# A hybrid decoder step: fp32r state update, early merge, and a group norm computed by halves

## The chip, the cores and the metric

The kernel runs on one core of one Trainium2 chip. The metric is the device time of one execution in microseconds. The engines are named as in the profile: PE is TensorE (PEld its weight loads), DVE is VectorE, ACT is ScalarE, POOL is GpSimd, SP is SyncE, which issues most DMAs.

## What is computed

One inference step of one decoder layer for 256 prompt tokens and 8 x 4 sample tokens (288 columns in all), D_MODEL 2048:

```
x += 0.5 * swiglu(rmsnorm(x));  x += mix(rmsnorm(x)) @ w_out;  x += 0.5 * swiglu(rmsnorm(x));  y = rmsnorm(x)

mix:  q, k, v, f, z, xbc, dt, g, u = split(xn @ w_in)
      att  = forgetting attention(q, k, v)                       # 512 features
      y, state = ssd_scan(x, dt, a, B, C, h0)                    # 16 heads x 64, state 128, 2 groups
      yg   = (y * silu(z)) in 2 groups of 512
      yg   = yg * rsqrt(mean(yg * yg) + eps) * ssd_norm          # the group norm
      lru  = rglru(u) * gelu(g)                                  # 512 features
      out  = [att | yg | lru] @ w_out
```

For the sample tokens the scan starts from `state_ssd` (8 sequences x 16 heads x 64 x 128, 4 MB), and the new states are an output.

## The kernel before

The residual x lies transposed in SBUF, 16 blocks of 128 features by 288 tokens. Every weight tile of 128 columns is loaded in fp32 (`wraw`, four slots), rounded to fp32r by ACT (`whi`), its remainder computed by DVE (`wlo`), and multiplied in three fp32r products per k-block (`products`, L792 to L794), so 48 products for 16 k-blocks. The activations are split in the same way (`xn_hi`/`xn_lo`, for the second half of the mixer `m_hi`/`m_lo`).

The mixer has 41 input tiles (`in`), then 16 output tiles of part 0 (k-blocks of attention and LRU, held in blocks 0 to 3 and 12 to 15 of `xn_hi`), 24 products each, then 16 of part 1 (the eight normed SSM blocks). The order is written by hand: the list `STEPS` is walked by each engine in its own program, and each step issues what that engine has to do for it. Beside the tiles stand these steps:

- `turn_x` transposes the conv output (`xsT`) to token rows (`xsn`, `bnat`), in three blocks of tokens; block 2 holds the 32 sample tokens, copied into two row groups (`turn_copies`, L824).
- `scores` makes the masked C B products (`cbm`), `hist` turns the conv histories, `ssd` h makes head h's decay matrix (`lseg` on DVE and ACT, `mseg` on POOL) and, for odd h, the output y of two heads back (`ssd_y`).
- `merge` rounds attention and LRU into `xn_hi`/`xn_lo`; `decay_s` makes the sample rows of `bexp` (B masked by sequence).
- `unit` i turns 4 x 2 heads of the old state (`ht`, L817), computes the update of unit i-1 (L1084, K = 32 rows, fp32) and its contribution to y (L1088). ACT copies `h0t`, DVE writes `snew`, SP stores it and loads the state four units on (`load_h0`).
- `gate_prompt` multiplies y by silu(z) on DVE and squares it on ACT; `sum_prompt` sums the squares over features on PE with a matrix of ones (L1102).
- `carry` finishes the sample columns; `groups` 0 to 3 compute mean, root (Ln, then Exp on ACT, then a Newton step on DVE), norm and rounding for both groups at once.
- `decay_x` and `state` make the prompt's final state.

PE writes the side products of all steps to three PSUM banks in turn: `JOB` numbers them in the order of STEPS, and `claim` for job j waits until job j-3 was read by its reader.

The old state's four slots (`h0`) lie in `xn_lo` blocks that the input tiles use, and SP loads them only after `merge` (wait for `merged` 8). The lines of the steps after the input tiles are, before:

```
    STEPS += [("hist", 2), ("hist", 3)] + ssd(2) + tile()
    STEPS += ssd(2) + [("in", IN_TILES), ("merge", 0)]
    STEPS += [("decay_s",)]
    for n, h in enumerate(heads):
        j, odd = h // 2 - 2, h % 2
        STEPS += [("ssd", h), ("unit", next(units)), ("sum_prompt" if odd else "gate_prompt", j)]
        STEPS += out() if n % 3 != 2 else []
```

## Time and profile before

| | us |
|---|---|
| three timed runs | 2293.6, 2294.14, 2295.75 (median 2294.14) |
| the profiled execution's own time | 2286.04 |
| its span, first to last instruction | 2284.9 |
| PE busy in the span | 2219.1 (97%) |
| DVE busy | 1194.9 (52%) |
| ACT busy | 820.2 (36%) |
| POOL busy | 155.9 (7%) |
| mean granted TensorE clock | 0.990 of full speed |

The profiled execution and the timed runs are different executions; the first is a little shorter than the median of the second. A matmul's duration in the timeline includes its way through the array, so products that follow each other overlap: what one costs is the distance from its start to the next one's. An fp32 matmul stands in two records. The granted clock of a window is 1.00 for 2.4 GHz all through and 0.50 for 1.2 GHz all through. The profile calls the state's slots `h`.

### The profile page before, as it was taken

Reading aid. Unit: us, or ns where it says so; the run is one execution under the profiler, and the core shown is the slowest. Engines: PE = TensorE matmul, PEld = TensorE weight load, DVE = VectorE, ACT = ScalarE, POOL = GpSimd, SP = SyncE. Lnnn points to the kernel's source line nnn. Section 1 sums busy time; section 2 is a strip of 40 time slices with the busy share of each in tenths; the row PEclk is TensorE's granted clock in tenths of the full one; section 3 lists DMA queues with packets and bytes.
Section 4 is the critical chain, followed back from the end, with each engine's and each line's share of the span. In section 5 each row is a group of like instructions: output and inputs, shape, how many; then the busy total and the mean of one; then the engine's idle time right before and its main releaser. Section 6 shows DMA issues by size and latency. Waiting matters only on the chain.

```text
span 2284.9 us, 41945 instructions
## 1 busy us (share of the span) xinstructions
PE 2219.1 (97%) x17040; PEld 2154.8 (94%) x17040; DVE 1194.9 (52%) x1541; ACT 820.2 (36%) x798; POOL 155.9 (7%) x221
## 2 busy tenths in 40 slices
PE   6999999999999999999999899899999999999998
PEld 6999999999999999988888679899999999999997
DVE  5555445554445457556436666545444554445554
ACT  5333233333233343344343435433333333233333
POOL 2410000000000030100000202000000000000022
PEclk8999999999999999999999999999999999999999
DMA  7665665656666566656975555665566656566552
GB/s 190 172 169 153 166 167 163 167 159 170 166 166 164 148 163 198 184 165 187 287 220 176 165 148 172 169 166 163 158 167 165 168 157 167 161 166 166 158 158 93
DMA packets 696130, 386.51 MB, mean 169 GB/s; under 512 B 18216, under 2 KB 677836, under 8 KB 695192
## 3 DMA queue, kind: packets, MB, share of 16 engines
q1 hardware_dynamic: 691528, 378.79, 60.0%
q0 software_dynamic: 4112, 5.94, 1.0%
q8 instruction: 75, 1.23, 0.2%
q10 hardware_dynamic: 384, 0.30, 0.0%
q14 instruction: 31, 0.25, 0.0%
HBM read 373.86 MB, written 11.13 MB: 168 GB/s over the span
## 4 chain that ended last, share of the span: by engine, by line
PE 88%; DVE 4%; SPq 2%; ACT 2%; issue 2%; DMA 1%; ACTq 0%; POOL 0%; DVEq 0%; POOLq 0%
PE bank L792 28%; PE bank L794 28%; PE bank L793 28%; DVE wlo L1524 1%; SPq L488 1%; PE bank L817 1%; SPq L487 1%; PE bank L1084 1%; ACT whi L1208 1%; PE bank L999 0%; DMA kpage<-cache_k 0%; DMA vpages<-cache_v 0%; DVE xn_lo L1514 0%; PE bank L945 0%; PE bank L944 0%
## 5 line engine op out<-in xcount | busy, mean ns | idle before, releaser
L792 PE MATMUL bank<-xn_hi,whi 128*128 128x288 f32 x3536 | 1057.2, 299 | 22.3 <-DVE xn_lo L1514 10.8
L793 PE MATMUL bank<-xn_hi,wlo 128*128 128x288 f32 x3536 | 1047.9, 296 | 0.0
L794 PE MATMUL bank<-xn_lo,whi 128*128 128x288 f32 x3536 | 1044.2, 295 | 0.0
L1524 DVE TENSOR_TENSOR wlo<-wraw,whi 128x2048 fp32r<-128x2048 f32 (+3 forms) x341 | 726.5, 2130 | 391.6 <-ACT whi L1208 391.2
L1208 ACT CAST whi<-wraw 128x2048 fp32r<-128x2048 f32 (+3 forms) x341 | 605.4, 1776 | 748.0 <-PE bank L794 740.9
L792 PEld LDWEIGHTS bank<-xn_hi,whi 128*128 128x128 f32 x3536 | 667.6, 189 | 29.9 <-DVE wlo L1524 17.7
L794 PEld LDWEIGHTS bank<-xn_lo,whi 128*128 128x128 f32 x3536 | 670.7, 190 | 0.0
L793 PEld LDWEIGHTS bank<-xn_hi,wlo 128*128 128x128 f32 x3536 | 668.8, 189 | 0.3
L794 PE MATMUL bank<-h_lo,whi 128*128 128x288 f32 x1376 | 407.0, 296 | 0.0
L792 PE MATMUL bank<-h_hi,whi 128*128 128x288 f32 x1376 | 406.1, 295 | 0.0
L793 PE MATMUL bank<-h_hi,wlo 128*128 128x288 f32 x1376 | 404.9, 294 | 0.0
L793 PEld LDWEIGHTS bank<-h_hi,wlo 128*128 128x128 f32 x1376 | 259.1, 188 | 0.0
L792 PEld LDWEIGHTS bank<-h_hi,whi 128*128 128x128 f32 x1376 | 258.3, 188 | 0.0
L794 PEld LDWEIGHTS bank<-h_lo,whi 128*128 128x128 f32 x1376 | 258.0, 188 | 0.0
L1222 ACT ACTIVATE sg<-sg 128x288 f32<-128x288 f32 x86 | 38.3, 445 | 422.8 <-DVE sg L1532 422.8
L1558 DVE SCALAR_TENSOR_TENSOR xT<-bank,xT 128x288 f32 (+1 forms) x108 | 49.5, 458 | 207.3 <-PE bank L794 207.3
L1532 DVE TENSOR_TENSOR sg<-bank,rs 128x288 f32<-128x288 f32 x86 | 39.4, 458 | 179.6 <-PE bank L794 179.5
L632 POOL COPY ssum<-sq 128x288 f32<-128x288 f32 x3 | 3.9, 1297 | 1415.3 <-ACT sq L1199 1415.3
L1539 DVE TENSOR_TENSOR hm<-bank,rs 128x288 f32<-128x288 f32 x86 | 39.3, 457 | 114.0 <-PE bank L794 114.0
L639 POOL TENSOR_TENSOR ssum<-ssum,sq 128x288 f32<-128x288 f32 x45 | 68.3, 1519 | 134.8 <-ACT sq L1199 134.8
L1547 DVE TENSOR_TENSOR h_lo<-hm,h_hi 128x288 f32 (+1 forms) x86 | 39.4, 459 | 9.0
L817 PE MATMUL bank<-ident,kpage 128*128 128x128 f32 x256 | 35.0, 280 | 6.8 <-DMA kpage<-cache_k 3.9
(355 smaller groups left out, 1136.1 us busy)
## 6 DMA issues: line engine op xcount, KB each, us to landing
wraw<-ffn_w_gate SPq DMA_DIRECT2D x86, 1024.0 KB, 5.9
wraw<-ffn_w_up SPq DMA_DIRECT2D x86, 1024.0 KB, 5.8
wraw<-ffn_w_down SPq DMA_DIRECT2D x64, 960.0 KB, 5.5
wraw<-w_in SPq DMA_DIRECT2D x40, 1024.0 KB, 6.3
wraw<-ffn_w_down SPq DMA_DIRECT2D x32, 832.0 KB, 5.2
kpage<-cache_k SPq DMA_DIRECT2D x64, 256.0 KB, 3.0
vpages<-cache_v SPq DMA_DIRECT2D x64, 256.0 KB, 4.0
wraw<-w_out SPq DMA_DIRECT2D x64, 256.0 KB, 3.4
```

The source lines that it names most:

```text
L639: pool.tensor_tensor(ssum[:], ssum[:], sq[:, odd, :], ALU.add).then_inc(sem("summed"), 1)
L792: pe.matmul(out, hi, rhs_hi, start=k == 0, stop=False)
L793: pe.matmul(out, lo, rhs_hi, start=False, stop=False)
L794: return pe.matmul(out, hi, rhs_lo, start=False, stop=k == nk - 1)
L817: return pe.transpose(out, src, ident[0:n, 0:n])
L1208: act.copy(tile_ap(whi, (base + j) % 2, nk), tile_ap(wraw, slot, nk)).then_inc(sem("hi_done"), 1)
L1222: act.activation(sg[:, par, :], sg[:, par, :], ACT.Silu).then_inc(sem("silu_done"), 1)
L1524: dve.tensor_tensor(tile_ap(wlo, s, nk), tile_ap(wraw, (base + j) % LOADS, nk), tile_ap(whi, s, nk).bitcast(F32), ALU.subtract).then_inc(s ...
L1532: dve.tensor_tensor(sg[:, par, :], bank[bk][:, 0:N], rs[:, 2, :], ALU.mult).then_inc(sem("scaled"), 1)
L1539: dve.tensor_tensor(hm[:, par, :], bank[bk][:, 0:N], rs[:, 2, :], ALU.mult).then_inc(sem("up_scaled"), 1)
L1547: dve.tensor_tensor(h_lo[:, bass.ds(slot, 1), :].rearrange("p o t -> p (o t)"), hm[:, par, :], h_hi[:, bass.ds(slot, 1), :].rearrange("p o ...
L1558: dve.scalar_tensor_tensor(out=xk, in0=bank[bk][:, 0:N], scalar=scale, in1=xk, op0=ALU.mult, op1=ALU.add).then_inc(sem("x_added"), 1)
```

## The change

Four things:

1. The sample rows of x and B are split into a rounded part and a remainder, each in its own row group of 32 (x: high, high, low, low; B: high, low, high, low), so that the update of the state is one fp32r product over 128 rows (`xw`, `bsp`, `masked_b`) in place of an fp32 one over 32.
2. The last input tile takes the outer k-blocks first (`LAST_K`), and `merge` stands ahead of heads 2 and 3; it waits for `outer_used`, which counts after the first eight k-blocks.
3. The old state's slots and `bexp` lie in the halves of `wraw` that output tiles leave free; SP loads them once the last input tile's remainder is done.
4. The group norm is done by halves. Group 0's `ys`, mean, root and norm (`ys_scale`, `ys_turn`, `mean`, `norm`, `round`) stand amid the units, group 1's at the end. POOL adds the squares of a group's four blocks, and PE multiplies one sum instead of four. ACT takes a square root, and DVE a reciprocal, in place of Ln and Exp.

Units begin two heads later, so three more of them follow each other behind the last head.

```diff
-    STEPS += ssd(2) + [("in", IN_TILES), ("merge", 0)]
+    STEPS += [("merge", 0)] + ssd(2) + [("in", IN_TILES)]
...
-    STEPS += [("decay_s",)]
+    NORM0 = {10: [("ys_scale", 0)], 11: [("ys_turn", 0)], 12: [("mean", 0)], 13: [("norm", 0)]}
     for n, h in enumerate(heads):
         j, odd = h // 2 - 2, h % 2
-        STEPS += [("ssd", h), ("unit", next(units)), ("sum_prompt" if odd else "gate_prompt", j)]
-        STEPS += out() if n % 3 != 2 else []
-    for u, more in zip(units, ([("gate_prompt", 7)], [("sum_prompt", 7)] + out(), [])):
-        STEPS += [("unit", u)] + more
-    STEPS += [("carry",)] + out() + [("groups", 0), ("decay_x",)] + out() + [("groups", 1)] + out() + [("groups", 2)] + out()
-    STEPS += [("state", 0), ("state", 1), ("groups", 3)] + out()
+        STEPS += [("ssd", h)] + ([("unit", next(units))] if n >= 2 else []) + [("sum_prompt" if odd else "gate_prompt", j)]
+        STEPS += out() if n < 2 or n % 3 != 1 else []
+        STEPS += [("decay_s",)] if n == 0 else NORM0.get(n, [])
+    STEPS += [("unit", next(units)), ("gate_prompt", 7), ("round", 0)] + out() + [("unit", next(units)), ("sum_prompt", 7)]
+    STEPS += [("unit", next(units))] + out() + [("unit", next(units)), ("decay_x",)] + out() + [("unit", u) for u in units]
+    STEPS += [("ys_scale", 1)] + out() + [("ys_turn", 1), ("state", 0)] + out() + [("mean", 1), ("state", 1)] + out()
+    STEPS += [("norm", 1), ("round", 1)]
...
SP:
-                        sp.wait_ge(sem("merged"), 8)
+                        sp.wait_ge(sem("lo_done"), IN0 + IN_TILES)
...
POOL:
+            elif what == "sum_prompt" and i % 4:
+                pool.wait_ge(sem("y_squared"), i + 1)
+                if i % 4 > 1:
+                    pool.wait_ge(sem("prompt_summed"), i // 4 * 3 + i % 4 - 1)
+                s = zT[:, i // 4 * 4, 0:NP_]
+                pool.tensor_tensor(s, s, zT[:, i, 0:NP_], ALU.add).then_inc(sem("prompt_summed"), 1)
...
PE:
+        LAST_K = [0, 1, 2, 3, 12, 13, 14, 15] + list(range(4, 12))
...
-                for k in range(KT):
+                for n, k in enumerate(LAST_K if t == IN_TILES - 1 else range(KT)):
...
+                    if t == IN_TILES - 1 and n == 7:
+                        last.then_inc(sem("outer_used"), 1)
...
-                if not (first and part == 0 and n < 2):
+                if first and part == 0 and n < 2:
+                    pe.wait_ge(sem("in_taken"), IN_TILES)
+                else:
                     pe.wait_ge(sem("x_added"), XO0 + part * KT + n + it4 - 1)
...
+                    if first and part == 1 and n == 0 and k in (0, 4):
+                        pe.wait_ge(sem("merged"), k + 12)
...
-                            m = turn_copies(to[:, c * P:(c + 1) * P], src, 1 if i < 2 else 2)
+                            m = turn_copies(to[:, c * P:(c + 1) * P], src, 1 if i < 2 else 4)
...
-                        pe.wait_ge(sem("bexp_ready"), 2)
-                        pe.matmul(to[:, :], xsn[SX, 2, c * P:(c + 1) * P], bexp[SX, c // 4, b0:b0 + 4, :],
+                        pe.wait_ge(sem("bexp_ready"), 4)
+                        pe.matmul(to[:, :], xw[:, c * P:(c + 1) * P], masked_b(c // 4, u % 2),
...
+                elif what == "mean":
+                    to = claim(pe, "mean", i)
+                    pe.wait_ge(sem("prompt_summed"), 3 * i + 3)
+                    pe.matmul(to[:, 0:NP_], ones[:], zT[:, 4 * i, 0:NP_], start=True, stop=True)
+                    pe.wait_ge(sem("gsq_ready"), i + 1)
+                    pe.matmul(to[:, NP_:N], ones[:], gsq[:, i, :], start=True, stop=True).then_inc(side_done("mean", i), 1)
...
ACT:
-                    act.wait_ge(sem("w_used"), IN0 + IN_TILES)
+                    act.wait_ge(sem("outer_used"), 1)
...
-                    act.activation(grs[:, 1], grs[:, 0], ACT.Ln).then_inc(sem("groot_step"), 1)
-                    act.wait_ge(sem("groot_step"), 1)
-                    act.activation(grs[:, 1], grs[:, 1], ACT.Exp, scale=-0.5).then_inc(sem("groot_step"), 1)
+                elif what == "mean":
+                    copied(act, "mean", i)
+                    act.activation(grs[:, 1, :], grs[:, 0, :], ACT.Sqrt).then_inc(sem("groot_step"), 1)
+                elif what == "round":
+                    if i == 0:
+                        act.wait_ge(sem("mseg_ready"), H_SSD)
+                        take(act, "y", 7)
+                    else:
+                        for q in range(2):
+                            act.wait_ge(sem(f"snew_stored{q}"), 16 * ND)
+                    act.wait_ge(sem("yn_done"), i + 1)
+                    act.copy(m_hi[:, 4 * i:4 * i + 4, :], zT[:, 4 * i:4 * i + 4, :]).then_inc(sem("m_rounded"), 1)
...
DVE:
+            def split_sample_x():
...
+                decay = nat[:, 2, 96 + 32:96 + 48]
+                dve.tensor_tensor(by_head(xw[:]), by_head(xsn[:, 2, :]), spread(decay, HD), ALU.mult)\
+                    .then_inc(sem("xw_step"), 1)
+                dve.tensor_copy(bsp[:], bnat[:, 2, :]).then_inc(sem("xw_step"), 1)
+                dve.wait_ge(sem("xw_step"), 1)
+                dve.tensor_tensor(by_head(xsn[low, 2, :]), by_head(xsn[low, 2, :]), spread(decay[low], HD), ALU.mult)\
+                    .then_inc(sem("xw_step"), 1)
+                dve.wait_ge(sem("xw_step"), 2)
+                for r in (1, 3):
+                    dve.tensor_tensor(bsp[SQ[r], :], bnat[SQ[r], 2, :], bsp[SQ[r], :].bitcast(F32), ALU.subtract)\
+                        .then_inc(sem("xw_step"), 1)
+                dve.wait_ge(sem("xw_step"), 3)
+                dve.tensor_tensor(xw[low, :], xsn[low, 2, :], xw[low, :].bitcast(F32), ALU.subtract)\
+                    .then_inc(sem("xw_step"), 1)
+                dve.wait_ge(sem("xw_step"), 6)
...
+                elif what == "mean":
...
+                    dve.tensor_scalar(v, src[:, 0:N], 1.0 / 512, EPS, ALU.mult, ALU.add).then_inc(side_read("mean", i), 1)
+                    dve.wait_ge(sem("groot_step"), i + 1)
+                    chain(dve.reciprocal(y, y))
+                    chain(dve.tensor_tensor(z, y, y, ALU.mult))
+                    chain(dve.scalar_tensor_tensor(out=z, in0=z, scalar=-0.5, in1=v, op0=ALU.mult, op1=ALU.mult))
+                    chain(dve.scalar_tensor_tensor(out=z, in0=z, scalar=1.5, in1=y, op0=ALU.add, op1=ALU.mult))
```

Where this puts the instructions is seen in the order on DVE at three places (the number after L is the line, before or after the change). First, behind the third block of `turn_x`; the parts of `xsn` and `bnat` are the turned rows, `cbm` the masked scores. Before:

```order
L1860 TENSOR_TENSOR xsn<-bank,nat 64x512 x2
L1865 COPY bnat<-bank 64x256
L1867 COPY cpad<-xsT 128x2x8x4
L1871 TENSOR_TENSOR cbm<-bank,tri 128x384
L1872 TENSOR_TENSOR cbm<-bank,tris 32x32
```

In the changed kernel:

```order
L1903 TENSOR_TENSOR xsn<-bank,nat 128x512 x2
L1908 COPY bnat<-bank 128x256
L1706 TENSOR_TENSOR xw<-xsn,nat 128x1024
L1708 CAST bsp<-bnat 128x256
L1710 TENSOR_TENSOR xsn<-xsn,nat 64x1024
L1714 TENSOR_TENSOR bsp<-bnat,bsp 32x256 x2
L1717 TENSOR_TENSOR xw<-xsn,xw 64x1024
L1912 COPY cpad<-xsT 128x2x8x4
L1916 TENSOR_TENSOR cbm<-bank,tri 128x384
L1917 TENSOR_TENSOR cbm<-bank,tris 32x32
```

Six instructions of the split now stand ahead of the first masked score.

Second, on DVE around the merge; `xn_lo<-attT` and `xn_lo<-gT` are its two subtractions, `lseg` a head's decay (three instructions), `zT<-bank` the read of an input tile. Before, from head 3 on:

```order
L1889 TENSOR_SCALAR lseg<-bank,nat 128x256
L1889 TENSOR_SCALAR lseg<-bank,nat 128x128
L1889 TENSOR_SCALAR lseg<-bank,nat 32x32
L1895 SCALAR_TENSOR_TENSOR xsT<-xsT,dcol,bank 128x288
L1647 TENSOR_TENSOR zT<-bank,rs 128x288
L1876 TENSOR_TENSOR xn_lo<-attT,xn_hi 128x1152
L1879 TENSOR_TENSOR xn_lo<-gT,xn_hi 128x1152
L1910 TENSOR_TENSOR xsn<-xsn,nat 32x1024
L1912 TENSOR_TENSOR bexp<-bnat,bmask 32x1024 x2
```

In the changed kernel, from the weight of output tile 0 to the read of the last input tile:

```order
L1539 TENSOR_TENSOR wlo<-wraw,whi 128x1024
L1921 TENSOR_TENSOR xn_lo<-attT,xn_hi 128x1152
L1924 TENSOR_TENSOR xn_lo<-gT,xn_hi 128x1152
L1934 TENSOR_SCALAR lseg<-bank,nat 128x256
L1934 TENSOR_SCALAR lseg<-bank,nat 128x128
L1934 TENSOR_SCALAR lseg<-bank,nat 32x32
L1934 TENSOR_SCALAR lseg<-bank,nat 128x256
L1934 TENSOR_SCALAR lseg<-bank,nat 128x128
L1934 TENSOR_SCALAR lseg<-bank,nat 32x32
L1940 SCALAR_TENSOR_TENSOR xsT<-xsT,dcol,bank 128x288
L1664 TENSOR_TENSOR zT<-bank,rs 128x288
```

The subtractions stand ahead of heads 2 and 3, and the read of the last input tile behind them all. The four products of `bexp` follow after head 4, the gating of y 0 and one more weight.

Third, on DVE, the first group's norm in the changed kernel; `grs` holds mean and root, `snew` is a unit's new state. Before, these `grs` steps (L1953 to L1963, 576 columns for both groups) stand after the last unit.

```order
L1999 TENSOR_SCALAR grs<-bank 128x288
L2001 RECIPROCAL grs<-grs 128x288
L2002 TENSOR_TENSOR grs<-grs 128x288
L2003 SCALAR_TENSOR_TENSOR grs<-grs 128x288
L2004 SCALAR_TENSOR_TENSOR grs<-grs 128x288
L1940 SCALAR_TENSOR_TENSOR xsT<-xsT,dcol,bank 128x288
L1967 SCALAR_TENSOR_TENSOR snew<-wraw,dec,bank 128x128 x4
L2007 SCALAR_TENSOR_TENSOR zT<-xsT,params,grs 128x288 x4
L1967 SCALAR_TENSOR_TENSOR snew<-wraw,dec,bank 128x128 x4
L1992 TENSOR_TENSOR xsT<-xsT,zT 128x256
L2013 TENSOR_TENSOR m_lo<-zT,m_hi 128x1152
L1637 TENSOR_TENSOR xT<-xT,bank 128x288
```

The read of y 7 (`xsT<-xsT,dcol,bank`) stands behind the whole root, and norm and rounding ahead of the addition of an output tile and the weight after it.

## Rows read from the trace of the kernel before

**Rows 1.** The page, part 1: busy us, share of the span and instructions
```profile
PE 2219.1 (97%) x17040; PEld 2154.8 (94%) x17040; DVE 1194.9 (52%) x1541; ACT 820.2 (36%) x798; POOL 155.9 (7%) x221
```

**Rows 2.** Waits of PE, 1225 to 1440 us: us in total, times, longest
```profile
PE bank L817 <- DMA h<-state_ssd: 10.4, 1, 10.4
...
PE bank L1096 <- DVE ys L1930: 2.2, 1, 2.2
PE bank L792 <- DVE wlo L1524: 2.0, 1, 2.0
```

**Rows 3.** Windows: length; busy of PE, PEld, DVE, ACT, POOL; granted clock; DMA
```profile
1268.00:1272.50 4.50, 4.42 (x20) 4.46 (x21) 2.37 (x6) 2.36 (x5) 1.21 (x2) 0.52 0.81 234
1353.00:1361.00 8.00, 7.74 (x38) 7.77 (x39) 3.72 (x7) 2.63 (x3) 0.00 (x0) 0.58 0.61 172
1367.00:1371.50 4.50, 4.50 (x22) 4.50 (x23) 4.36 (x7) 0.00 (x0) 0.00 (x0) 0.62 0.39 117
```

**Rows 4.** Timeline of PE: start, duration (us), line, out<-in, count [idle before]
```profile
1236.35 2.38 PE L824 MATMUL bank<-ident,xsT 128*32 128x128 f32 x40
...
1240.72 1.06 PE L817 MATMUL bank<-ident,histO 128*27 128x128 f32 x8
...
1249.50 0.29 PE L792 MATMUL bank<-xn_hi,whi 128*128 128x288 f32 x1
...
1255.88 0.43 PE L1057 MATMUL bank<-cshl,hot 128*128 128x288 f32 x2
...
1268.08 1.09 PE L817 MATMUL bank<-ident,h 128*128 128x128 f32 x4 [10.40 <-DMA h<-state_ssd]
1268.82 0.59 PE L792 MATMUL bank<-xn_hi,whi 128*128 128x288 f32 x1
...
1275.51 1.12 PE L1084 MATMUL bank<-bexp,xsn 32*128 32x512 f32 x2
1276.56 0.42 PE L1088 MATMUL bank<-h0t,cpad 128*32 128x128 f32 x8
1276.92 0.70 PE L1102 MATMUL bank<-zT,ones 128*128 128x256 f32 x2
...
1277.58 0.29 PE L793 MATMUL bank<-xn_hi,wlo 128*128 128x288 f32 x1
...
1382.26 0.37 PE L792 MATMUL bank<-m_hi,whi 128*128 128x288 f32 x1 [0.34 <-issue]
```

**Rows 5.** DVE, groups by form, 1233 to 1384: busy us, mean ns | idle before
```profile
L1524 DVE TENSOR_TENSOR wlo<-wraw,whi 128x1024 fp32r<-128x1024 f32 x18 | 22.6, 1258 | 11.7 <-ACT whi L1208 11.7
...
L1967 DVE SCALAR_TENSOR_TENSOR zT<-xsT,params,grs 128x288 f32<-128x288 f32 x8 | 3.5, 511 | 0.0
...
L1974 DVE TENSOR_TENSOR m_lo<-zT,m_hi 128x1152 fp32r<-128x1152 f32 x2 | 2.6, 1352 | 0.0
...
L1905 DVE TENSOR_TENSOR xsn<-xsn,nat 128x1024 f32<-128x1024 f32 x2 | 2.4, 1218 | 0.0
```

**Rows 6.** Timeline of DVE and POOL, 1251 to 1256 us
```profile
1251.73 3.39 POOL L738 TENSOR_TENSOR mseg<-lseg,cbm 128x384 f32<-128x384 f32 x4 [33.90 <-ACT lseg L1374]
...
1253.15 1.87 DVE L1524 TENSOR_TENSOR wlo<-wraw,whi 128x1024 fp32r<-128x1024 f32 x1 [1.88 <-ACT whi L1208]
```

**Rows 7.** DMA issues, 1225 to 1440 us: count, KB each, us to landing
```profile
xT<-x_save SPq DMA_DIRECT2D x1, 2304.0 KB, 8.5
```

**Rows 8.** Timeline of DVE around the first score mask
```profile
1239.80 0.56 DVE L1871 TENSOR_TENSOR cbm<-bank,tri 128x384 f32<-128x384 f32 x1 [0.35 <-PE bank L1050]
1240.27 0.17 DVE L1872 TENSOR_TENSOR cbm<-bank,tris 32x32 f32<-32x32 f32 x1
```

**Rows 9.** DVE, groups by form, whole span: the wide reciprocal
```profile
L1585 DVE RECIPROCAL ps<-ps 72x288 f32<-72x288 f32 x1 | 1.9, 1949 | 0.0
```

**Rows 10.** Timeline of ACT around the group norm's root
```profile
1362.74 1.28 ACT L1396 ACT_TABLE_LOAD   x1
1364.04 0.69 ACT L1396 ACTIVATE grs<-grs 128x576 f32<-128x576 f32 x1
```

166 lines of the change are left out of this document (74 added, 92 removed).

## Prediction

> **What bounds the kernel now.** I read the page first: TensorE (PE) is busy 97% of the span [rows 1], so time is to be had only where PE waits, runs at its lower clock, or does work that can be made cheaper. The changed code acts only in the second half of the mixer, from the turning of the third token block (about 1236 us) to the first output tile that uses the normed heads (1382.26). The waits of PE in that stretch come next [rows 2]: 10.4 us for the first load of the old state, 2.2 us for `ys`, 2.0 us for a rounded weight. Then the windows [rows 3]. After each of the three waits the granted clock reads 0.52, 0.58 and 0.62, which means that PE ran at the 1.2 GHz level for most of it. Window length times (1 - granted) gives what each cost: 4.5 x 0.48 = 2.2, 8.0 x 0.42 = 3.4, 4.5 x 0.38 = 1.7 us. So the waits of before cost 14.6 us and the slow stretches behind them 7.3 us. Last I read PE's own order [rows 4], with both ends of the stretch, for the price of each kind of work. Where a product follows a product, start to start is its cost: an input tile of 48 products takes 6.38 us (1249.50 to 1255.88), 0.133 each, and an output tile of 24 takes 3.2.
>
> **The change, part by part** (minus is faster).
>
> *State update as one fp32r product.* Per unit, L1084 takes 1.05 us (1275.51 to 1276.56) for 512 columns in fp32 [rows 4]. In fp32r, 0.133 us for 288 columns scales to 0.24. I take 0.24, since more rows in the contraction cost nothing in the 128-row tiles; the other bound is no gain, 1.05. 16 x 0.81 = -13.0. Not all of it comes through: two even heads are followed by an odd one with no tile between, and there the odd head's products wait for the side bank that ScalarE empties, as just met before; I give back 0.85 twice, +1.7.
>
> *Sums of squares on GpSimd.* Eight L1102 products go, two come. One costs about 0.53: 1276.92 to 1277.58, less one 0.133 product [rows 4]. 6 x 0.53 = -3.2, and +0.4 for two small sample products where one stood: -2.8. GpSimd's six sums lie beside other work: two heads' mseg took it 3.39 us [rows 6], a sum is narrower than one of the mseg products, and a head now takes PE about 4 us. Vector's (DVE's) weight subtraction L1524 took 1.87 us beside GpSimd's 3.39 us of mseg, against a mean of 1.26 [rows 5, 6], so six sums could slow DVE by 0 to 3.9 us. I take 0, since DVE has slack per head in the steady part. The Trainium skill (GPSIMD Engine Reference, key points) says that GpSimd shares its memory interfaces with VectorE and contends with instructions that have two SBUF inputs, which speaks against this move; it also puts elementwise work at about twice VectorE's time. By that rule the sum would be up to 3.9 worse; the 1.87 agrees with it.
>
> *Merge before heads 2 and 3, state loads free of it.* Before, head 4 ends at 1257.68 and PE idles until 1268.08 [rows 4]; its first output tile starts at 1268.8, 19.3 after the start T of the last input tile (1249.50). Now the outer k-blocks come first in that tile, done at T+3.2, and ScalarE, free of the next weight at T+3.6, rounds twice until T+5.7. DVE ends that weight at T+5.5 [rows 6], subtracts twice (1.35 each) until T+8.1, and only then does heads 2 and 3 (0.8 each), y 0 and the read of the tile (0.4 each): T+10.5, for which the output tile now waits. PE is free at about T+8, so a wait of 2.7 stands in place of 10.4: 19.3 - 10.5 = -8.8. The low clock behind it stays (+0.1). The loads of the state now queue behind the 2304 KB copy of x, 8.5 us [rows 7]; both end near T+14, and the first unit is at T+20: hidden.
>
> *Three-part split of the sample rows.* Each of ten chunks is turned into four row groups instead of two. Two copies cost 0.23 (2.38 us for ten) [rows 4]; four narrow products into four groups take 0.36 (L1088, 1276.56 to 1276.92): +1.3; the bounds are 0 and 2.4. DVE gets a chain ahead of the score masks: three products like L1905, 1.22 each [rows 5], and three of 256 columns, some 0.3 each by size: 4.6 us. The second history turn on PE needs the bank of score mask 0. That mask waited 0.35 and ended at 1240.44 [rows 8], 0.8 before that turn started (half-way through the row at 1240.72). So PE moves by 1.3 + 4.6 - 1.2 = +4.7, 3.2 of it idle, and I add a slow stretch of +2.0, between the 1.7 and 3.4 seen. The later weights are 3 us early and stay covered.
>
> *The mask product.* Four of 512 columns, 0.6 each, now stand on DVE after the weight of tile 1 and before head 5. Before, 3.5 us of it hid in the 10.4 wait. Tile 2's weight comes 2.0 later than PE wants it: +2.0, clock +1.7, and 0.2 at tile 1: +3.9.
>
> *First norm amid the units.* On DVE: scale and add, then ScalarE's root (0.5 with hand-over), a reciprocal of 1.95 (the 72x288 row of L1585 [rows 9]; cost goes by columns), three steps of about 0.5, as L1967 [rows 5]: 4.4 us in which DVE does nothing else. Behind it is the read of y 7, whose bank the next turn of the state needs: PE waits 3.0. Then four norm products, a rounding of 1.15 on ScalarE and a 1.35 subtraction [rows 5] stand before the weight of tile 11: 1.8 more, and clock 1.7: +6.5.
>
> *Tail.* The `ys` and weight waits and their clock go, -9.3. In their place: 0.8 at tile 13; and after the second mean product DVE needs 4.4 for the root, 1.6 for an addition and a weight, 2.0 norm, ScalarE 1.1, DVE 1.4, in all 10.4, against PE's 1.9 (state) + 3.2 (last tile) + 1.6 (first four k-blocks, already normed) = 6.7. Wait 3.7, clock 1.7: net -3.1.
>
> The removed logarithm pair had a table load of 1.28 between its two steps, 1362.74 to 1364.04 [rows 10]; with a square root none stands on the chain. The Trainium skill (ScalarE: Activation LUTs, What ACT_TABLE_LOAD costs) counts 2.66 us for each switch, a drain included. The row has the next activation right behind the 1.28, so here the drain is not seen, and by the page's figure the old chain would have been 1.4 longer; the sum uses the row.
>
> **Sum:** -13.0 + 1.7 - 2.8 - 8.7 + 6.7 + 3.9 + 6.5 - 3.1 = -8.8, about -9. The profiled execution took 2286.04 (span 2284.9), so it would take 2277; the three timed runs have a median of 2294.14, 8 above it, and -9 makes that 2285.
>
> **Rivals.**
> 1. *The new waits are dearer* (no change). I count five or six waits of 2 to 4 us, in place of one long and two short. If each is followed by 3.4 of lost clock and not 1.7 to 2.0, +8: 2293. For: one of the three did. Against: two did not.
> 2. *The waits are shorter* (faster still). If only the merge and the last root make PE wait long enough for the clock, the split, mask, and norm stretches give back 2.0 + 1.7 + 1.7 + some 2 of wait: 2278. For: steady heads leave DVE 2 us per three heads.
> 3. *The clock stays low between neighbouring waits* (slower). From the merge wait to tile 2 PE has 9.7 us of work between two waits, from the norm wait to tile 11 another 7, and the input tile after the split is 6.4. If all of it runs at 1.2 GHz, it takes twice as long and costs 23 where I counted 7.6: +15.5, and 2301. It decides from 13.6 us lost beyond the count on, that is, only if nearly every low stretch lasts until the next wait. Against: two of three ended within 4.5 us [rows 3].
> 4. *The fp32r product is no cheaper.* Then -8.8 + 13.0 - 1.7 = +2.5: 2297, inside what counts as the same by half of its chance. Against: every weight product of the kernel is fp32r at 0.133.
> The Trainium skill (TensorE: Matmul & The Clock Gate, What's actually happening) calls the lower clock the default, released by activity, which is the ground of rivals 1 and 3; its figures are not used.
>
> **How the numbers follow.** What this kernel's measurement tells from no change is about 0.2%, 4.6 us. Forecast 0.58 (about 2280 to 2289, all faster); rival 2 0.14; rival 1 0.18, mostly within 4.6 us; rival 3 0.06; rival 4 0.04. Faster 0.72, same 0.20, slower 0.08. The range leaves out rivals 3 and 4 and the ends: low 2277, from rival 2, high 2293, from rival 1 and the bounds of the turning (+1.1) and of GpSimd's contention.
>
> **What would show it.** State updates of about 0.24 us start to start; mean products twice; PE's long wait for the load of the old state gone, one of 2 to 3 us before output tile 0; a new PE wait of about 3 before the second history turn; a wait at the turn of the state near head 17 on the y bank; a wait of about 3.7 before the fifth k-block of the first second-half tile. The mixer from 1249.50's tile to that tile should take 117 us, not 132.8. I am wrong if the split costs PE nothing or twice 6.7, or if windows behind the waits keep a granted clock near 0.5 for over 8 us.

## The result, and the profile after

| | us |
|---|---|
| the changed kernel, 20 runs | median 2285.41 (2279.64 to 2293.02) |
| the kernel before, 20 runs beside them | median 2290.27 (2285.99 to 2297.80) |
| ratio of the two, with its 95% interval | 0.9975 (0.9965 to 0.9984), that is 5.7 us less (3.7 to 8.0) |

The forecast of 2285 and "faster" came true; the size of the gain did not quite. The forecast counted 9 us down from 2294.14, the median of three runs. The twenty runs put the kernel before at 2290.27, and the change took off 5.7.

The profiled executions of the two kernels have the same span, 2284.9 us, and still the stage that the change touches is shorter. From here on *the stage* is the way from the first turning of the convolution's output (the first of its three token blocks) to the first product of the second feed-forward. It contains every instruction that the change moves. Before, it took 203.2 us (1233.30 to 1436.48), after it 195.1 (1237.55 to 1432.67): 8.1 less.

The rest of the span, where PE runs the same work, was 8.1 us longer in this one execution. It is the clock: outside the stage running below full clock cost PE 6.1 us before and 15.7 after, with its waits equal and its work the same within 1.6 (the mean granted clock of the whole span was 0.990 and 0.986). Such differences are common here: in thirteen profiles with this same code ahead of the stage, its start lay anywhere from 1230.6 to 1242.5. So the experiments below are read by two things, the stage and the ratio of many runs.

The two do not agree fully. The runs give 5.7 us (3.7 to 8.0) where the stage gives 8.1, and of the twelve kernels below eleven also gain less by the runs than by the stage, by 0.5 to 4.7 us. The kernel before has one profile only, so whether its stage was long in it, or the changed kernels lose time elsewhere, stays open. Against each other the changed kernels are on firmer ground.

The page of the changed kernel, part 1: busy us, share of the span and instructions.

```profile
PE 2214.6 (97%) x17066; PEld 2159.1 (94%) x17066; DVE 1204.8 (53%) x1555; ACT 818.9 (36%) x798; POOL 161.1 (7%) x227
```

PE is busy 4.5 us less than in [rows 1], DVE 9.9 more, POOL 5.2 more (six sums of 0.73, the rest longer `mseg` products). The waits of PE in the stage of the changed kernel (us in total, times, longest) stand where [rows 2] stood:

```profile
PE bank L803 <- DVE wlo L1539: 4.8, 5, 2.1
PE bank L830 <- DVE cbm L1917: 3.8, 1, 3.8
PE bank L830 <- DVE xsT L1940: 3.1, 1, 3.1
PE bank L803 <- DVE m_lo L2013: 2.6, 1, 2.6
PE bank L892 <- ACT h0t L1398: 1.5, 2, 0.7
PE bank L803 <- issue: 1.2, 1, 1.2
PE bank L1103 <- DVE lseg L1934: 1.2, 3, 0.6
PE bank L1076 <- DVE lseg L1934: 1.1, 1, 1.1
```

The one long wait for the load of the old state and the two short ones have become fifteen shorter ones, 19.3 us in all against 14.6 (14.9 with one of 0.3 that names `issue`). Twelve of the fifteen name DVE. The windows of the changed kernel (columns as in [rows 3]) show the granted clock behind five of them, and the recovery after the last:

```profile
1249.40:1252.40 3.00, 2.99 (x13) 2.86 (x14) 0.88 (x3) 1.90 (x2) 0.00 (x0) 0.51 0.08 21
1269.70:1273.00 3.30, 3.28 (x14) 3.30 (x15) 1.31 (x4) 3.27 (x3) 1.45 (x4) 0.52 1.19 305
1282.50:1287.00 4.50, 4.43 (x22) 4.44 (x23) 2.77 (x7) 2.36 (x5) 2.01 (x4) 0.62 0.00 0
...
1339.60:1345.00 5.40, 4.74 (x28) 4.12 (x29) 4.68 (x15) 1.23 (x3) 0.15 (x1) 0.68 0.36 99
...
1378.50:1384.00 5.50, 5.50 (x30) 5.50 (x31) 3.08 (x4) 1.82 (x3) 0.40 (x1) 0.69 0.32 95
1384.00:1390.00 6.00, 6.00 (x48) 6.00 (x47) 3.62 (x7) 3.51 (x6) 1.39 (x2) 1.00 0.52 152
```

Length times (1 - granted) gives 1.5, 1.6, 1.7, 1.7 and 1.7 us: five stretches near the 1.2 GHz level, each over within about 5 us, 8.2 in all against the 7.3 of before. Forecast were five of 1.7 to 2.3, 9.4 in all. So the stage splits in three: the waits grew by 4.6 (15.2 to 19.7, counting every one over 0.15 us but the last), the low clock took 0.9 more, and PE's own work, which is what remains of 203.2 and 195.1, fell by 13.5, from 180.7 to 167.2. PE gained more by cheaper work than it lost in waits. *Work* below always means this remainder.

Where the 8.1 us come from, by five marks on PE (T is the start of the last input tile):

| us | before | after | difference | forecast |
|---|---|---|---|---|
| first turning to T | 16.20 | 21.55 | +5.35 | +6.7 |
| T to the first output tile | 19.32 | 10.62 | -8.70 | -8.7 |
| first output tile to the first product with normed heads | 113.44 | 104.33 | -9.11 | -12.2 |
| from there to the second feed-forward | 54.22 | 58.62 | +4.40 | +5.4 |
| the stage | 203.18 | 195.12 | -8.06 | -8.8 |

Each interval came out within 1.4 us but the third, 3.1 off, where the update, the sums, the mask and the first norm meet. The experiments take these apart.

### The profile page after: what moved, and what is told of

The parts are those of the page before. It is cut to its first block, busy times and chain, and to the rows that moved or that the text cites. A ratio compares the mean times of both kernels' runs of the same rounds, so it can differ in the third digit from the quotient of the medians.

```text
span 2284.9 us, 42031 instructions
## 1 busy us (share of the span) xinstructions
PE 2214.6 (97%) x17066; PEld 2159.1 (94%) x17066; DVE 1204.8 (53%) x1555; ACT 818.9 (36%) x798; POOL 161.1 (7%) x227
## 4 chain that ended last, share of the span: by engine, by line
PE 85%; DVE 6%; SPq 3%; ACT 2%; issue 2%; DMA 1%; ACTq 0%; POOL 0%; DVEq 0%; POOLq 0%
PE bank L803 28%; PE bank L805 27%; PE bank L804 27%; DVE wlo L1539 1%; SPq L492 1%; SPq L491 1%; ACT whi L1221 1%; PE bank L830 1%; DMA vpages<-cache_v 0%; PE bank L1018 0%; DMA kpage<-cache_k 0%; DVE snew L1967 0%; DVE lseg L1934 0%; PE bank L1185 0%; DVE xn_lo L1529 0%
## 5 line engine op out<-in xcount | busy, mean ns | idle before, releaser
L803 PE MATMUL bank<-m_hi,whi 128*128 128x288 f32 x128 | 38.8, 303 | 3.7 <-DVE m_lo L2013 2.6
```

What stands on the lines that cost most here:

```text
L803: pe.matmul(out, hi, rhs_hi, start=nth == 0, stop=False)
```

## Experiments

All run as changes of the changed kernel (195.1 us, ratio 0.9975). Every ratio is against the kernel before, from runs side by side; before ran at medians of 2289.06 to 2290.41. Two rows that differ by less than about 0.0015 (3.4 us) are not told apart by the runs alone. The stage comes from one profile each: in e3, e4, e5, e7 and e9 0.7 to 1.3 us of it lie ahead of T, at the same waits, and are the clock of that execution.

| run | stage | ratio, 95% interval |
|---|---|---|
| e1, split behind the scores | 189.9 | 0.9953 (0.9937 to 0.9969) |
| e2, each update product twice | 198.3 | 0.9978 (0.9965 to 0.9990) |
| e3, first mean one step later | 197.7 | 0.9987 (0.9976 to 0.9998) |
| e4, update product in fp32 | 199.4 | 1.0004 (0.9993 to 1.0015) |
| e5, sums back on PE | 197.2 | 0.9989 (0.9980 to 0.9998) |
| e6, root by logarithm | 194.8 | 0.9975 (0.9965 to 0.9984) |
| e7, merge behind the heads | 196.9 | 0.9975 (0.9964 to 0.9987) |
| e8, update all as before | 198.9 | 0.9991 (0.9977 to 1.0006) |
| e9, e4 and e7 together | 201.7 | 1.0002 (0.9988 to 1.0015) |
| e10, e1 with the mask in halves | 188.1 | 0.9952 (0.9938 to 0.9966) |
| e13, its second half a step earlier | 188.7 | 0.9950 (0.9932 to 0.9968) |
| e14, and the root apart | 190.2 | 0.9947 (0.9931 to 0.9963) |

One of the twelve runs of e14 took 4306.15 us at a full granted clock. It is left out of its ratio, and its cause is not known.

**The split (e1).** In the changed kernel DVE makes the three parts of x before the score masks. Timeline of DVE in the changed kernel:

```profile
1243.74 1.23 DVE L1706 TENSOR_TENSOR xw<-xsn,nat 128x1024 fp32r<-128x1024 f32 x1
1244.88 0.29 DVE L1708 CAST bsp<-bnat 128x256 fp32r<-128x256 f32 x1
1245.20 1.22 DVE L1710 TENSOR_TENSOR xsn<-xsn,nat 64x1024 f32<-64x1024 f32 x1
1246.45 0.86 DVE L1714 TENSOR_TENSOR bsp<-bnat,bsp 32x256 fp32r<-32x256 f32 x2
1247.35 1.22 DVE L1717 TENSOR_TENSOR xw<-xsn,xw 64x1024 fp32r<-64x1024 f32 x1
...
1248.72 0.55 DVE L1916 TENSOR_TENSOR cbm<-bank,tri 128x384 f32<-128x384 f32 x1
1249.18 0.17 DVE L1917 TENSOR_TENSOR cbm<-bank,tris 32x32 f32<-32x32 f32 x1
```

The chain takes 1243.74 to 1248.57, 4.8 us (forecast 4.6), and the mask behind it is what PE waits for. PE's timeline there, in the changed kernel:

```profile
1240.60 2.39 PE L837 MATMUL bank<-ident,xsT 128*32 128x128 f32 x80
1242.92 2.13 PE L1069 MATMUL bank<-xsT 128*128 128x256 f32 x12
1244.98 0.62 PE L830 MATMUL bank<-ident,histO 128*27 128x128 f32 x4
1249.41 1.05 PE L830 MATMUL bank<-ident,histO 128*27 128x128 f32 x4 [3.81 <-DVE cbm L1917]
```

e1 moves the call, and nothing else:

```
 turn_x, third block (DVE):
-                    if i == 2:
-                        split_sample_x()
 scores (DVE), after the masks:
+                    split_sample_x()
```

> The three-part split moves on VectorE from ahead of the masked scores to behind them, so that the second history turn no longer waits for it. Stage here and below: from the first turn of the conv output (1233.30 us before, 1237.55 in the changed kernel) to the first product of the second feed-forward (1436.48 and 1432.67): 203.2 us before, 195.1 changed. Theory 1 (the split's only price is the 3.8 us wait and the low clock of 2.3 us after it, some 1.5 lost; behind the scores VectorE waits anyway, 2.4 and 2.7 us): the wait goes, stage 190 (-5.3), total about 0.2% under the changed kernel, near 0.995 of the kernel before. Rival (the split is on VectorE's path wherever it stands): the wait moves to the last input tile's weight or to heads 0 and 1, and the stage stays within 1.5 us of 195.

Measured: stage 189.9, first turning to T 16.22, as the theory had it. The wait for `cbm` is gone from PE's waits, and nothing waits for the split at its new place. So 5.2 us were spent for an order that nothing asked for: the first reader of the parts is the mask product on DVE at 1276.35, 28 us after the chain ended. The ratio of the runs says the same, 0.9953 for 0.9975, 5.0 us.

**The price of the update product (e2).**

```
+                        pe.matmul(to[:, :], xw[:, c * P:(c + 1) * P], masked_b(c // 4, u % 2), start=True, stop=True)
                         pe.matmul(to[:, :], xw[:, c * P:(c + 1) * P], masked_b(c // 4, u % 2), start=True, stop=True)
```

> Each of the 16 fp32r state updates is issued twice into the same bank; the result is the same. The changed kernel's trace shows 0.41 us from the start of a 512-column update to the start of the next product, where the sum on record had 0.24. Theory 1 (0.41 is what such a product costs): 16 x 0.41 = 6.6, less what disappears in waits for the h0t copy and for heads' decay (some 1.5), stage 200 (+5). Rival (0.24 is the price of the product, the rest is a fixed gap to the fp32 products behind it, paid once): 16 x 0.22 = 3.5, less 1, stage 197.5 (+2.5).

Timeline of PE in e2, one unit (start, duration):

```profile
1289.30 0.47 PE L1103 MATMUL bank<-bexp,xw 128*128 128x512 f32 x1
1289.62 0.39 PE L1105 MATMUL bank<-bexp,xw 128*128 128x512 f32 x1
1289.93 0.42 PE L1109 MATMUL bank<-h0t,cpad 128*32 128x128 f32 x8
```

A unit in the changed kernel, and one before (turn of the state, update, its contribution to y):

```profile
1301.42 0.60 PE L830 MATMUL bank<-ident,wraw 128*128 128x128 f32 x4
1301.77 0.48 PE L1103 MATMUL bank<-bexp,xw 128*128 128x512 f32 x1
1302.18 0.42 PE L1107 MATMUL bank<-h0t,cpad 128*32 128x128 f32 x8
...
1280.77 0.60 PE L817 MATMUL bank<-ident,h 128*128 128x128 f32 x4
1281.30 1.12 PE L1084 MATMUL bank<-bexp,xsn 32*128 32x512 f32 x2
1282.35 0.42 PE L1088 MATMUL bank<-h0t,cpad 128*32 128x128 f32 x8
```

Two products take 0.63 us from the first start to that of the fp32 products behind them (1289.30 to 1289.93), one takes 0.41 (1301.77 to 1302.18). So the second costs 0.22, the rival's price, and the forecast's 0.24 for a product among its like was about right. The other 0.19 of the 0.41 come once, at the passage to the fp32 products. Against that the update now starts 0.35 after the turn ahead of it (1301.42 to 1301.77) and before it started 0.53 after it. From the turn to the products behind the update a unit took 1.58 and takes 0.76, 0.82 less.

PE's work grew by 3.6 (0.22 to 0.24 a unit). The waits gave back 2.0: the two for `h0t` fell from 0.74 to 0.53 each, the one for the y bank from 3.1 to 2.7, and most of the short ones for `lseg` went. The low stretch behind the y bank was twice as long in this execution and took 1.5 more, which makes the 3.2 that reached the stage. It lies between theory and rival, nearer the rival. In the runs e2 is 0.7 us slower than the changed kernel (0.9978 for 0.9975), inside both intervals.

**The update in fp32 (e4).** Same operands, same 128 rows, no fp32r:

```
-                        pe.matmul(to[:, :], xw[:, c * P:(c + 1) * P], masked_b(c // 4, u % 2),
+                        pe.matmul(to[:, :], xw[:, c * P:(c + 1) * P].bitcast(F32),
+                                  masked_b(c // 4, u % 2).bitcast(F32),
```

> Only the 16 products of the state update lose their fp32r form: they run as plain fp32 over the same 128 rows and 512 columns, and compute the same. Theory (the cheaper product carries 10 us of the stage): each goes from 0.31 to 0.41 us back to about 1.05, so the stage from the first turn of the convolution's output to the first product of the second feed-forward grows from 195.1 by 16 x 0.64 to 0.74 = 10 to 12 us, to 205 to 207. Rival (the time stood under cover of the vector engine, and the saving was small): the stage grows by under 5 us, to 200 at most.

Measured: the product takes 0.95 to 1.06, and with a slower start behind the turns PE's work is 10.4 us more from the first output tile to the first normed product. The stage grew by 4.3, 1.0 of it ahead of T, so 3.3 are the update's: the rival, by this one execution. Where 10.4 went shows in the waits of PE in e4:

```profile
PE bank L803 <- DVE wlo L1540: 3.8, 3, 2.1
PE bank L830 <- DVE cbm L1918: 3.8, 1, 3.8
PE bank L803 <- DVE m_lo L2014: 2.6, 1, 2.6
PE bank L830 <- DVE xsT L1941: 2.3, 1, 2.3
...
PE bank L1103 <- DVE lseg L1935: 0.8, 2, 0.6
```

The waits for `h0t` (1.5) are gone, those for `wlo` are 1.0 shorter, for the y bank 0.9, for `lseg` 0.5: 3.8 by their hundredths. The rest is clock. The windows of e4 behind tile 2 and behind the y bank, where the changed kernel had 0.62 and 0.68:

```profile
1284.50:1289.00 4.50, 4.49 (x41) 4.16 (x41) 2.76 (x7) 2.37 (x5) 1.98 (x4) 1.00 0.00 0
1344.80:1350.30 5.50, 5.48 (x42) 4.53 (x43) 4.08 (x13) 1.97 (x4) 0.74 (x1) 1.00 0.51 135
```

Length times (1 - granted) these two low stretches had cost the changed kernel 1.7 us each. 10.4 - 3.8 - 3.4 = 3.2, against 3.3 seen. So part is cover: DVE and ACT set the pace among the units once the product is cheap, and 3.8 of the 10.4 us go into waits for them. The other part is the clock of this execution and no property of the dear product: e9 has the same product and the same wait of 2.3 us for the y bank, and a low stretch behind it. The runs agree: e4's ratio is 1.0004 for 0.9975, 6.6 us more, which is 10.4 - 3.8 with the clock left out; their intervals allow 3 to 10.

**The update all as before (e8):** fp32, 32 rows of contraction, two copies in the turning, no split.

```
-            pe.matmul(to[:, :], xw[:, c * P:(c + 1) * P], masked_b(c // 4, u % 2),
+            pe.matmul(to[:, :], xsn[SX2, 2, c * P:(c + 1) * P], masked_b(c // 4, u % 2)[SX2].bitcast(F32),
...
```

> The state update is done as in the kernel before (plain fp32 products over 32 rows, two copies in the turning, x unsplit), all else as in the changed kernel; the result is the same. Theory (as e4_update_fp32 showed, two thirds of the dearer products lie under waits for VectorE and ScalarE, and the split's 5.3 us before the last input tile is gone as in e1_split_late): from the changed kernel's 195.1 the stage goes by -5.3 + 4.3 to 194, within 1.5 of it. Rival (the update's 10 us count in full): the stage is 200 or more.

Measured 198.9, 1.1 short of the rival and 4.9 above the theory, which took over e4's low stage. Both expectations missed. The split's 5.3 went as in e1; against e1 it is 9.0 more in the stage and 8.7 by the ratios. That is what the cheap update is worth against the one of before, both without the split in the way: 11.8 us of PE's work, less 1.5 that go into waits and 1.4 of clock. It is more than e4 tells, in part since the 32-row product of before is dearer than e4's (below). From the third output tile to the first normed product e8 took 100.7 us, the changed kernel 91.5, e4 94.8. The 6 us between e8 and e4, with the same arithmetic, are for the most part two stretches of low clock that e4 did not have. Windows of e8 at tile 2 and behind the y bank:

```profile
1279.40:1284.00 4.60, 4.54 (x23) 4.55 (x24) 2.81 (x7) 2.36 (x5) 2.01 (x4) 0.63 0.00 0
1341.80:1348.50 6.70, 6.70 (x27) 4.48 (x28) 4.69 (x14) 2.69 (x4) 0.73 (x1) 0.51 0.49 133
```

They cost 1.7 and 3.3 us. The waits ahead of them are 2.2 and 2.1 us; in e4 waits of 2.1 and 2.3 at the same places had nothing behind them. The 32-row product takes 1.05 each time where the 128-row one mostly took 0.95, and its start behind the turns 0.1 more. What decides whether the clock falls after a wait of 2 us these runs do not settle.

**The sums of squares (e5).**

```
 POOL:
-                pool.tensor_tensor(s, s, zT[:, i, 0:NP_], ALU.add).then_inc(sem("prompt_summed"), 1)
 PE, each prompt block:
+                    pe.matmul(bank[4][:, g * NP_:(g + 1) * NP_], ones[:], zT[:, i, 0:NP_], start=i % 4 == 0, stop=i % 4 == 3)
...
```

> Only the sums of squares of the prompts' columns go back to TensorE (six products with ones), out of GpSimd; the result is the same. Theory (the forecast's term of 2.8 us): each product takes about 0.44 to 0.46 us on TensorE, so the stage grows from 195.1 by 2.6 to 2.8, to about 197.8. Rival (GpSimd's sums slow VectorE beside them and give that back): the stage stays within 1 us of 195.1, and VectorE's busy time in it falls by 1 us or more.

Measured 197.2, +2.1, by the ratios +3.2 (0.9989 for 0.9975): nearer the theory. PE's work grew by 2.6, 0.43 for each of six sums. 0.7 of the stage's 2.1 lie ahead of T, and against that the waits for `wlo` are 0.9 shorter. POOL's sums do not slow DVE: the 34 subtractions for `wlo` took 1308 ns on average in the changed kernel's stage and 1306 in e5's, and DVE was busy 138.5 and 138.6 us. What contends is the pair of `mseg` products, and these stand in both kernels. Groups of DVE by form in the changed kernel, 1262 to 1374 (busy us, mean ns | idle before):

```profile
L1992 DVE TENSOR_TENSOR xsT<-xsT,zT 128x256 f32<-128x256 f32 x8 | 6.0, 750 | 1.0 <-ACT zT L1284 1.0
```

The gate product of y took 416 ns before (L1946), 750 now, 749 in e5 and 504 in e4. It slows not through the sums but because, with the cheap update, it falls beside POOL's `mseg`: four of the eight took 1.07 to 1.10 us (the first on DVE at 1295.27, POOL's pair at 1295.07), the others 0.40 to 0.43. The Trainium skill (GPSIMD Engine Reference, Specifications) says that the two engines contend where VectorE's instruction has two SBUF inputs; this product has, and the trace agrees.

**The merge (e7).**

```
-    STEPS += [("merge", 0)] + ssd(2) + [("in", IN_TILES)]
+    STEPS += ssd(2) + [("in", IN_TILES), ("merge", 0)]
```

> The merge stands behind heads 2 and 3 again, all else as changed (outer k-blocks first, state loads early, mask products late). Theory 1 (the order buys what stood before the merge on ScalarE: heads, table load, silu): the two subtractions end 15.3 after the start of the last input tile, as before, and output tile 0 starts there and not at 10.6: stage 200 (+4.7). Rival (the gain at the merge came from the state load and the mask products alone, which before stood between 15.3 and 19.3, and the read of the last input tile holds the output tile anyway): stage within 1 of 195.

Measured: stage 196.9, +1.8, where the theory had +4.7 and the rival less than 1. T to the first output tile is 14.2 instead of 10.6, so the early merge is worth 3.6 of the 8.7 there. The other 5.1 came without it; what else was changed at this place is the state's load, which no longer waits for the merge, and the mask product, which moved behind it. No run parts these two. Of the 3.6 only 1.8 are left at the end of the stage, and 1.0 of that lies ahead of T and has nothing to do with the merge. The rest went behind the first output tile: in e7 the waits for `wlo` at tiles 1 and 2 are smaller, none and 0.8 in place of 0.8 and 2.0. Waits of PE in e7:

```profile
PE bank L803 <- DVE xn_lo L1921: 6.0, 1, 6.0
...
PE bank L803 <- DVE wlo L1539: 2.8, 4, 1.1
```

In the runs no difference is left: both ratios are 0.9975, with room for 3 us either way.

**Two undone together (e9).** The edits of e4 and e7.

> Two parts undone together: the update's products as plain fp32 over 128 rows (as e4_update_fp32) and the merge of h back behind the first two heads and the last input tile (as e7_merge_behind_heads). Theory (each alone costs 4.3 and 1.8 us of the stage, most of it hidden by other waits; together they use up cover at different places, so the two add up): 195.1 + 6.1 = 201.2, within 1.5. Rival (both were hidden behind the same waits, and with both gone it shows): 204 or more.

201.7 against 201.2 by adding, the theory: their losses lie at different places. By the ratios (1.0002) it is as e4 alone, which agrees with a merge worth nothing.

**The first norm (e3, e6).**

```
 e3:
-    NORM0 = {10: [("ys_scale", 0)], 11: [("ys_turn", 0)], 12: [("mean", 0)], 13: [("norm", 0)]}
+    NORM0 = {10: [("ys_scale", 0)], 11: [("ys_turn", 0)], 13: [("mean", 0), ("norm", 0)]}
 e6:
-                    act.activation(grs[:, 1, :], grs[:, 0, :], ACT.Sqrt)
+                    act.activation(grs[:, 1, :], grs[:, 0, :], ACT.Ln)
+                    act.activation(grs[:, 1, :], grs[:, 1, :], ACT.Exp, scale=-0.5)
 ...
-                    chain(dve.reciprocal(y, y))
```

> The first group's mean and root move behind head 17 and its unit, so that VectorE reads y 7 and writes a new state before the 4.4 us root. Theory 1 (the 3.1 us wait is a matter of order: the y bank stands behind the root): that wait goes, the weight of tile 11 comes at most 1.5 later, stage 193 (-2). Rival (VectorE has too much work in these steps, whatever the order): the wait turns up at the weights of tiles 10 and 11, stage within 0.7 of 195.

> Only the root of the group norm is taken as before, by a logarithm and an exponential on ScalarE, in place of a square root and VectorE's reciprocal. Theory (the reciprocal's 1.95 us is what holds the y bank of tile 7): the chain from the mean to the first read of that bank is 0.45 + 1.28 (a table load) + 0.45 = 2.2 us in place of 0.45 + 1.95 = 2.4, where the load is not hidden, and 0.9 where it is: the wait of 3.1 us for that bank falls to 1.6 to 2.9, stage 193.6 to 195. Rival (each switch of tables costs ScalarE more, and delays the copies of heads and the weights behind it): the wait goes over to a copy of ScalarE, stage 195.5 to 197.

Timeline of DVE in the changed kernel, the first mean, with the read of the y bank behind it:

```profile
1335.26 0.45 DVE L1999 TENSOR_SCALAR grs<-bank 128x288 f32<-128x288 f32 x1
1336.22 1.95 DVE L2001 RECIPROCAL grs<-grs 128x288 f32<-128x288 f32 x1 [0.51 <-ACT grs L1408]
1338.21 0.46 DVE L2002 TENSOR_TENSOR grs<-grs 128x288 f32<-128x288 f32 x1
1338.70 0.46 DVE L2003 SCALAR_TENSOR_TENSOR grs<-grs 128x288 f32<-128x288 f32 x1
1339.19 0.46 DVE L2004 SCALAR_TENSOR_TENSOR grs<-grs 128x288 f32<-128x288 f32 x1
1339.69 0.52 DVE L1940 SCALAR_TENSOR_TENSOR xsT<-xsT,dcol,bank 128x288 f32<-128x288 f32 x1
```

4.4 us from the mean to the read, as forecast. In e3 the chain stands elsewhere: PE's 3.1 for the y bank is gone, and 2.0 for `snew` and 2.6 for an `h0t` stand in its place; the stage is 2.5 longer, 1.0 of it ahead of T, the runs 2.7 (0.9987 for 0.9975). Neither expectation had that. e6 takes the same time as the reciprocal, the upper end of its theory. Timeline of ACT in e6:

```profile
1333.00 1.28 ACT L1408 ACT_TABLE_LOAD   x1
1334.64 0.44 ACT L1408 ACTIVATE grs<-grs 128x288 f32<-128x288 f32 x1 [0.36 <-DVE grs L2001]
1335.10 1.28 ACT L1410 ACT_TABLE_LOAD   x1
1336.40 0.44 ACT L1410 ACTIVATE grs<-grs 128x288 f32<-128x288 f32 x1
```

The second load costs 1.30 in the chain, the reciprocal that it replaces 1.95, and the exponential 0.44: the wait for the y bank became 2.9 in place of 3.1, the stage 194.8, the ratio the same. The Trainium skill (ScalarE: Activation LUTs, What ACT_TABLE_LOAD costs) counts a drain with each switch, 2.66 us in all; between the end of the first activation and the start of the next stand 1.32 here, so the drain is not seen.

**The mask in halves, and the root apart (e10, e13, e14)**, all with e1's order.

```
 e10, e13 (5 in place of 6 in e13):
-        STEPS += [("decay_s",)] if n == 0 else NORM0.get(n, [])
+        STEPS += [("decay_s", 0)] if n == 0 else [("decay_s", 1)] if n == 6 else NORM0.get(n, [])
 ... (PE's first eight updates wait for group 0's two products alone)
 e14, beside e13's:
-    NORM0 = {10: [("ys_scale", 0)], 11: [("ys_turn", 0)], 12: [("mean", 0)], 13: [("norm", 0)]}
+    NORM0 = {10: [("ys_scale", 0)], 11: [("ys_turn", 0)], 12: [("mean", 0)], 13: [("root", 0), ("norm", 0)]}
-    ... ("mean", 1), ("state", 1)] + out()
+    ... ("mean", 1), ("state", 1), ("root", 1)] + out()
```

> As e1_split_late, with VectorE's four products of the decay with the mask in two parts: group 0's two where all four stood, group 1's two behind the sixth unit; TensorE's products of group 0 wait for the first part alone. Theory (the wait of 2.1 us at tile 2 comes from the 2.7 us of the four products): it falls by the 1.3 us of two, and if the granted clock then stays up beside it, by another 1 to 1.7; the stage goes from e1_split_late's 189.9 to 187 to 188.6. Rival (another thing is late next at tile 2, or the second part delays a unit later): the stage stays at 189.5 to 190.5.

> As e10_mask_halves, with the second part of VectorE's mask products one step earlier, behind the low part of an output tile's weights, where VectorE waited 1.1 us for TensorE. Theory (the part's 1.3 us then lie in that wait): the wait of 1.5 us before an update product goes back to 0.3 to 0.5, and from the first turn to the group norm's first product of the output, 131.0 in e10_mask_halves, it is 128.9 to 129.4. Rival (the part makes another step late there): 130.1 or more, no better than e1_split_late.

> As e13_mask_second_at_5, with the reciprocal and its three small steps taken out of the mean's step and put behind the eighteenth head and its unit for the first group, and behind the second state store for the second; the result is the same. Theory (the 3.1 us wait for the y bank is the 1.95 us reciprocal with its three steps of 0.46, 3.3 us in all, standing ahead of VectorE's read of that bank): the wait falls to under 0.5, and the work is then 3.3 us later, before the norm, where it may show in other waits; the way from the first turn to the group norm's first product shortens by 1 to 3 us against e13_mask_second_at_5. Rival (VectorE is full there, the wait only moves to the weights or to a copy of h behind it, as in e3_mean0_late): it shortens by under 1 us or grows.

e10 starts tile 2's products 1.2 us earlier, as expected, and loses 1.2 when the second half (1.28 on DVE) makes an update product wait 1.5 in place of 0.3, then 1.0 more on the way to the normed heads. e13 takes that wait away, keeps its 1.2 until PE's wait at 1316, and loses 1.4 behind it, where the clock fell. The window of e13 where it went:

```profile
1317.30:1321.80 4.50, 4.50 (x32) 4.45 (x28) 2.20 (x5) 0.77 (x1) 0.64 (x2) 0.77 0.63 174
```

The wait ahead of it is 0.6 us, the same as in e1, where the clock stayed up. From the first turning to the first normed product e1, e10 and e13 took 130.1, 131.0 and 130.3: no gain, which for e13 is the rival. e10's stage of 188.1 is inside its theory's range, but by the clock: behind the first normed product, with the same code and the same waits, e1, e10 and e13 took 59.9, 57.1 and 58.4, since the low stretch at the fifth k-block was long in e1 and did not come in e10. In e14 the y bank is read in time and PE is 4.6 us ahead of e13 there. 12 us further on it is 1.3 behind, after these waits and 6.8 us of low clock behind them. Waits of PE in e14:

```profile
PE bank L1103 <- ACT h0t L1398: 2.6, 1, 2.6
...
PE bank L830 <- DVE snew L1966: 1.5, 1, 1.5
```

Rival again: DVE has 4 us of norm to do among the units, wherever it is put. The four kernels with the late split have medians of 2281.67, 2279.04, 2279.15 and 2276.48 (e14 without its long run), ratios 0.9947 to 0.9953, and each one's interval holds the others. All of them beat the one before, and each is 5 to 6.4 us under the changed kernel, though the intervals of the first three still touch its interval; which of the four is best is not settled.

## Why the prediction was right, and where not

The direction and the mechanism by places held. That the time came out at 2285 is luck in part: two errors met. The base of 2294.14 was 3.9 above the median of the twenty runs, and the gain was 5.7 (3.7 to 8.0), where 8.8 was forecast; from 2290.27 the forecast would have been 2281.5. In the stage, -8.1 for -8.8, by the forecast's own steps:

- *State update, -13.0 + 1.7.* The step that was mis-sized. Start to start the product costs 0.41, not 0.24, since the passage to the fp32 products behind it costs 0.19 (e2), so the products save 10.2. The turns ahead of them, which start the update sooner now, save another 1.0, which the forecast did not have. In all PE's work is 12.0 less than with the old update (e8): the 13.0 were close. What comes back was put too low: the waits among the units (`h0t`, `lseg`) are 2.7, not 1.7, and 1.0 and 0.9 of the waits for the weights and the y bank, which the forecast booked under the mask, the norm and the tail, are there because the product is cheap (e4). So the update is worth 6.6 against e4's fp32 product and 9.0 against that of before (e8 against e1, 8.7 by the runs), where 11.3 were forecast.
- *Sums of squares, -2.8.* 2.6 on PE, 2.1 to 3.2 by e5. The contention that was weighed does not come from the sums (1308 and 1306 ns for a weight's subtraction with and without them); it is real and another's: `mseg` against the gate product, brought by the update's new pace.
- *Merge, -8.7.* -8.70 measured, step by step nearly: the tile starts at T + 10.62 for a forecast of T + 10.5. But the sentence that gives the merge the credit is wrong: e7 leaves next to nothing of it.
- *Split, +6.7.* +5.35. Four copies in place of two cost nothing (2.39 against 2.38), not 1.3; the idle time was 3.8, not 3.2 (4.6 - 1.2, its own terms, give 3.4); the low clock 1.5, not 2.0. e1 shows the whole term was to be had back by order.
- *Mask, +3.9.* Waits of 0.77 and 2.05 and a low stretch of 1.7, 4.5: right.
- *First norm, +6.5.* Wait 3.13 for 3.0, clock 1.7 for 1.7; behind it 0.24 and 0.66 in place of 1.8. 5.8 in all: right.
- *Tail, -3.1.* The wait at the first normed product 1.12 for 0.8, before the fifth k-block 2.57 for 3.7, clock 1.7 for 1.7: -9.3 + 5.4 = -3.9.

With the measured sizes: -10.2 - 1.0 + 2.7 - 2.6 - 8.7 + 5.35 + 4.5 + 5.8 - 3.9 = -8.05, against -8.06. The total came out close because errors cancelled: the update's two terms were 2.8 too good (-8.5 for -11.3), the split, the tail and the norm 2.9 too dear.

Of the signs that the forecast named, the wait before output tile 0 (1.13 and 1.25, with one record between), the one before the second history turn and the one on the y bank came. The update is not at 0.24 start to start, and the wait before the fifth k-block is 2.57. The 117 us from T count in +5.4 that are paid only at that k-block; to there 119.4 were measured, 1.9 of it the products ahead of it in the tile. To the first normed product, where the 132.8 of before end, the forecast's terms give 111.9, and 114.95 was measured.

The rivals: 1 and 2 differ by the length of the waits and the clock, and both came out at the forecast (8.2 us of low clock against 9.4). 3 is refuted for this profile: each low stretch ended within some 5 us, and the granted clock was 1.00 again before the next wait. 4 is refuted: 0.41 against 1.05.

## What to carry to other kernels

When PE's work is made cheaper in a stage where other engines follow closely, count what waits for them will take back: here 10.4 us of work were worth about 6.6 (e4), and 11.8 about 9 (e8 against e1). Before a new chain is put on an engine, ask who reads it first and what is queued behind it: this change gained 8.1 us and gave away 5.2 by a chain that stood 28 us ahead of its first reader. A wait that is taken away with its work merely moved on the same full engine came back at the next reader here (e3, e10, e14).

## What was not expected of the hardware

- Eighty narrow records of turning into four row groups took 2.39 us, forty into two 2.38. The Trainium skill (TensorE: Matmul & The Clock Gate, Part 3: Packing small matmuls) says that small-M products whose outputs lie in different groups of 32 partitions run concurrently; the trace agrees, and all four copies are here for the price of two.
- The granted clock does not fall after the same wait each time. At the y bank it fell after a wait of 3.1 us (changed kernel), 2.3 (e9) and 2.1 (e8), not after 2.3 (e4). At tile 2 it fell after 2.05 in the changed kernel and not in e1 or e4. In e13 it fell after 0.6, where in e1 it stayed. With the wait for `cbm` at 3.81 in each profile that has it, the way from the first turning to T varied from 21.55 to 22.84 us. With equal waits the way from the first normed product to the second feed-forward varied from 57.1 to 59.9. So 1 to 3 us of any stage here are chance, and a difference of that size wants many runs.
- A full fp32 reciprocal of 128x288 took 1.95 us on DVE, where a product of that shape took 0.46.
